# Convolution taps of the latent passes shared out anew over three engines, rope read from PSUM, Sigmoids moved to the end, and another order of the merge's products

## What is computed

```python
def conv_branch(p_glu, dw, dw_b, ln_g, ln_b, w_o):
    a, g = jnp.split(p_glu, 2, axis=-1)
    u = a * jax.nn.sigmoid(g)
    u = dwconv1d(u, dw, dw_b)              # 31 taps, depthwise, 512 channels
    u = jax.nn.silu(layernorm(u, ln_g, ln_b))
    return u @ w_o

h = modulate(rmsnorm(x, norm1_g[l]), sh1, sc1)
p = h @ w_in[l]
q, k, v = (split_heads(u) for u in jnp.split(p[..., GLU_END:QKV_END], 3, axis=-1))
q = rope_2d(q, pos_row, pos_col)
k = rope_2d(k, pos_row, pos_col)
y_conv = conv_branch(p[..., :GLU_END], ...)
y_attn = merge_heads(neighbourhood_attention(q, k, v, k_c, v_c, na_rpb[l])) @ w_na_out[l]
x = x + g1 * gated_merge(p[..., QKV_END:], y_conv, y_attn, w_out[l])   # gates: sigmoid
```

## Time and profile before

| | us |
|---|---|
| median of three executions | 2962.23 (2959.38 to 2964.63) |
| profiled execution, its own time | 2951.68 |
| its span | 2949.4 |
| TensorE busy | 2816.3 (95%) |
| VectorE busy | 1537.3 (52%) |
| ScalarE busy | 1116.2 (38%) |
| GpSimd busy | 1274.6 (43%) |

### The profile page before, as it was taken

One profiled execution on the slowest core, in us unless ns is written; L12 is line 12 of the kernel. 1 busy time (PEld: TensorE's weight loads), 2 busy tenths in 40 slices (PEclk: granted clock), 3 DMA queues, 4 the chain that ended last, 5 costly groups with the idle time before them and its releaser, 6 DMA issues.

```text
span 2949.4 us, 41217 instructions
## 1 busy us (share of the span) xinstructions
PE 2816.3 (95%) x15658; PEld 2297.0 (78%) x15658; DVE 1537.3 (52%) x1968; ACT 1116.2 (38%) x1666; POOL 1274.6 (43%) x696
## 2 busy tenths in 40 slices
PE   7999988999999999989999999999989999999998
PEld 6975734878888877867777888888877777788887
DVE  6865585353323255278775432423355867552525
ACT  4445223333323233236633422322343573342433
POOL 3444101435445173388842322222347784444443
PEclk9999998999999999999999999999999999999999
DMA  4235497323233233432222212122223222333332
GB/s 174 95 101 212 135 314 250 95 93 100 91 95 99 93 123 122 143 93 83 68 86 65 72 55 74 57 65 65 72 86 114 76 68 72 100 93 94 99 94 78
DMA packets 116008, 306.88 MB, mean 104 GB/s; under 512 B 36176, under 2 KB 44496, under 8 KB 115344
## 3 DMA queue, kind: packets, MB, share of 16 engines
q1 hardware_dynamic: 87584, 284.49, 30.5%
q10 hardware_dynamic: 27712, 18.50, 2.2%
q0 software_dynamic: 560, 1.84, 0.2%
HBM read 294.95 MB, written 7.45 MB: 103 GB/s over the span
## 4 chain that ended last, share of the span: by engine, by line
PE 77%; DVE 8%; DVEq 4%; ACT 3%; issue 2%; POOL 2%; DMA 2%; ACTq 1%; SPq 0%; POOLq 0%
PE ps L304 38%; PE ps L338 17%; PE ps L329 6%; PE ps L1941 3%; DVEq L2241 2%; POOL wlo L265 2%; DVE co L2240 2%; PE ps L2352 2%; PE ps L1945 1%; PE ps L1946 1%; PE ps L1949 1%; DMA mt<-ka 1%; PE ps L748 1%; DVE nacc L451 1%; PE ps L1999 1%
## 5 line engine op out<-in xcount | busy, mean ns | idle before, releaser
L265 POOL TENSOR_TENSOR wlo<-wraw,whi 128x1024 fp32r<-128x1024 f32 x373 | 923.1, 2484 | 1360.7 <-ACT whi L257 1359.3
L257 ACT ACTIVATE whi<-wraw 128x1024 fp32r<-128x1024 f32 x373 | 392.3, 1055 | 458.2 <-PE ps L304 170.5
L304 PE MATMUL ps<-xah,whi 128*128 128x512 f32 x992 | 387.9, 391 | 1.7 <-issue 1.7
L304 PE MATMUL ps<-xal,whi 128*128 128x512 f32 x992 | 387.4, 391 | 0.0
L304 PE MATMUL ps<-xah,wlo 128*128 128x512 f32 x992 | 280.1, 391 | 0.0
L2240 DVE SCALAR_TENSOR_TENSOR co<-ub,vec,co 128x512 f32<-128x512 f32 (+1 forms) x216 | 247.7, 1186 | 5.4 <-issue 0.4
L304 PEld LDWEIGHTS ps<-xah,whi 128*128 128x128 f32 x992 | 186.1, 188 | 42.8 <-issue 2.7
L304 PEld LDWEIGHTS ps<-xal,whi 128*128 128x128 f32 x992 | 186.1, 188 | 40.3
L304 PEld LDWEIGHTS ps<-xah,wlo 128*128 128x128 f32 x992 | 186.1, 188 | 40.2
L2339 POOL TENSOR_TENSOR co<-co,ct 128x512 f32<-128x512 f32 (+1 forms) x144 | 168.1, 1167 | 21.7 <-issue 1.8
L304 PE MATMUL ps<-hhi,whi 128*128 128x512 f32 x408 | 159.3, 390 | 1.1 <-ACT whi L257 1.1
(11 more groups left out here) (419 smaller groups left out, 6065.1 us busy)
## 6 DMA issues: line engine op xcount, KB each, us to landing
wraw<-stream SPq DMA_DIRECT2D x425, 512.0 KB, 3.5
wada<-w_ada SPq DMA_DIRECT2D x56, 512.0 KB, 7.4
wraw<-w_ada SPq DMA_DIRECT2D x40, 512.0 KB, 3.9
biasb<-attn_bias ACTq DMA_DIRECT2D x32, 256.0 KB, 3.6
xin<-x0T SPq DMA_DIRECT2D x4, 528.0 KB, 6.7
s_u<-uk ACTq DMA_DIRECT2D x8, 264.0 KB, 2.5
res<-x0T ACTq DMA_DIRECT2D x1, 2048.0 KB, 9.5
outT<-res SPq DMA_DIRECT2D x4, 512.0 KB, 2.6
```

Of the source, the lines that this page charges most:

```text
L257: act.activation(whi[:, s], wraw[:, s], ACT.Copy).then_inc(hi_done[s], 1)
L265: pool.tensor_tensor(wlo[:, s], wraw[:, s], whi[:, s].bitcast(F32), ALU.subtract).then_inc(lo_done[s], 1)
L304: last = pe.matmul(ps[:, bank, 0:b - a], w[:, s, kt], x[:, kt, c0 + a:c0 + b], start=start, stop=stop)
```

## The change

It has these parts. `rt`, the buffer of the rope's second product, is gone: the product with sin stays in PSUM bank 3 and is read from there, and the blocks between windows are written by additions of their own where they were copied. Taps in the latent passes: VectorE does tiles 1, 2 and 3 (`p.tiles`), GpSimd only adds tile 0's products, which ScalarE makes (`product_act`, into the one buffer `ct`), over all 30 taps. The context pass keeps GpSimd's two tiles. The first ten gates are read out with Copy, and their Sigmoids run in place beside the last units. The layer norm uses the bank of unit M + 3, and that unit's convolution half is begun last; in the context pass each unit now ends by itself. In `kv_act` one root moves behind a copy. TensorE gets 8 idle-time products (`keep_busy`, L505 before) at the end of the first network's S5 stage and 4 ahead of its first output projection.

```diff
@@ s5_pe
             if i in ADA_END:
                 pe.wait_ge(f_a.sem, f_a.past("bat", min(i + 2, NT - 1)))
+                if i == NT - 1:
+                    keep_busy(pe, 1, 8)
                 ada_turn(pe, ADA_END[i])
@@ class Pass
-            self.taps = KTAP if self.one else POOL_TAPS
+            self.taps = KTAP
+            self.tiles = (2, 3) if self.one else (1, 2, 3)
@@ kv_act
-        norm_root_act(act, n, then.T, "eps6")
         for j in range(4):
             ...
             act.activation(kctx[:, j], ps[:, s, 0:p.T], ACT.Copy).then_inc(acc_free[s], 1)
+            if j == 0:
+                norm_root_act(act, n, then.T, "eps6")
@@ evac_act
-            act.activation(gt[:, h, 0:p.T], a, ACT.Sigmoid).then_inc(acc_free[s], 1)
+            act.activation(gt[:, h, 0:p.T], a, ACT.Sigmoid if g >= p.U + 30 else ACT.Copy).then_inc(acc_free[s], 1)
@@ new in mix
+    def product_act(act, p, k):
+        if k > 1:
+            act.wait_ge(p.c_g.sem, p.c_g.past("conv", k - 2))
+        act.activation(ct[:, 0:p.T], ub[:, 0, k:k + p.T], ACT.Copy, scale=colr(f"dw{p.l}", 1, k * 4)).then_inc(p.c_t.sem, 1)
+    def products_of(n):
+        if n < 0:
+            return range(1, 5)
+        first = 5 + n + n // 2
+        return range(first, min(first + 1 + n % 2, KTAP))
@@ mix_act
             for g in late:
                 evac_act(act, p, g)
+            mine = list(products_of(n)) if p.lat else []
+            if mine:
+                product_act(act, p, mine[0])
             if 0 < n <= p.N:
                 copied_act(act, p, n - 1)
             if n < p.N:
                 exps_act(act, p, n)
+                if mine[1:]:
+                    product_act(act, p, mine[1])
...
         for g in range(p.U + 29, p.U + 36):
             evac_act(act, p, g)
+            d = 2 * (g - p.U - 29)
+            for h in range(d, min(d + 2, 30 - GATE0)):
+                act.activation(gt[:, h, 0:T], gt[:, h, 0:T], ACT.Sigmoid)
@@ post_dve
-            dve.tensor_tensor(rt[:, :], ps[:, 3, :], sinT, ALU.mult)
+            t = ps[:, 3, :]
+            dve.tensor_tensor(t, t, sinT, ALU.mult)
...
-                for m_, (lo, hi) in MIX.items():
-                    dve.tensor_copy(kT[:, m_ * P:m_ * P + 64], kT[:, lo * P:lo * P + 64])
-                    ins = dve.tensor_copy(kT[:, m_ * P + 64:m_ * P + P], kT[:, hi * P + 64:hi * P + P])
+                for m_, (lo, hi) in MIX.items():
+                    keys(m_ * P, 16 * (lo - 2), 8)
+                    ins = keys(m_ * P + 64, 16 * hi + 8, 8)
@@ mix_dve
         dve.wait_ge(p.c_g.sem, p.c_g.past("conv", p.taps - 2))
-        conv_taps(dve, p, range(p.taps, KTAP), (0, 1))
@@ mix_pool, latent passes
+            for n in range(-1, p.N + 2):
+                if n >= 0:
+                    split_lo(pool, p.U + 15 + n)
+                for k in products_of(n):
+                    if n < 0 and k < 4:
+                        split_lo(pool, p.U + 11 + k)
+                    o = co[:, 0, 0:T]
+                    pool.drain()
+                    pool.wait_ge(p.c_t.sem, p.c_t.past("t", k - 1))
+                    pool.tensor_tensor(o, o, ct[:, 0:T], ALU.add).then_inc(p.c_g.sem, 1)
@@ merge_pe
-        pe.wait_ge(acc_free[M % R], read_out(M - R))
+        pe.wait_ge(acc_free[(M + 3) % R], read_out(M - 1))
         conv_mean_pe(pe, p)
...
-        for kt in range(4):
-            pe.wait_ge(p.c_h.sem, p.c_h.past("hi", kt))
-            for j in range(1, R):
-                last = hi_part(j, kt)
-                if p.one and kt == 3:
-                    counted(j, last)
-            ...
-                last = hi_part(0, kt)
-                if p.one and kt == 3:
-                    counted(0, last)
+        for kt in range(2):
+            pe.wait_ge(p.c_h.sem, p.c_h.past("hi", kt))
+            for j in range(R - 1):
+                hi_part(j, kt)
+            ...
+        if p.one:
+            pe.wait_ge(p.c_h.sem, p.c_h.past("hi", 3))
+            for j in range(R):
+                for kt in range(2 if j < R - 1 else 0, 4):
+                    last = hi_part(j, kt)
+                counted(j, last)
+        else:
+            ...
+            for j in range(R - 1):
+                counted(j, lo_part(j, 3))
             for kt in range(4):
-                last = lo_part(0, kt)
-            counted(0, last)
-            for j in range(1, R):
-                counted(j, lo_part(j, 3))
+                last = lo_part(R - 1, kt)
+            counted(R - 1, last)
@@ the order of TensorE's work
             ssd_pe(pe)
+            keep_busy(pe, 5, 4)
             raw_pe(pe, U_OUT1, "ssd", ...)
```

More of the change, by code:

```diff
@@ L46 @@
 PADT = KTAP // 2
-POOL_TAPS = 22
 PHASES_DVE = 3
@@ L1830, in __init__ @@
             self.c_g = s("conv_taps", "conv", passes=self.taps - 1)
+            self.c_t = s("conv_products", "t", passes=self.taps - 1 if lat else 0)
             self.a_s, self.a_max, self.a_exp, self.a_rec, self.a_sc, self.a_turn, self.a_pt, self.a_pv = (
@@ L2142, in mix_act @@
             evac_act(act, p, g)
+            if p.lat:
+                product_act(act, p, g - p.U - 7)
+        if p.lat:
+            product_act(act, p, 4)
         late = [p.U + 8 + PRE - 1]
@@ L2167, in mix_act @@
         act.wait_ge(p.c_p.sem, p.c_p.past("var"))
-        act.activation(lst[:, 0, 0:T // P], ps[:, p.U % R, 0:T // P], ACT.Sqrt, bias=col("eps6")).then_inc(p.c_a.sem, 1)
+        act.activation(lst[:, 0, 0:T // P], ps[:, (p.U + 3) % R, 0:T // P], ACT.Sqrt, bias=col("eps6")).then_inc(p.c_a.sem, 1)
         for m in range(4):
@@ L2195, in post_dve, with keys @@
             dve.tensor_tensor(x, x, cosT, ALU.mult)
-            dve.tensor_tensor(rt[:, :], ps[:, 3, :], sinT, ALU.mult)
+            t = ps[:, 3, :]
+            dve.tensor_tensor(t, t, sinT, ALU.mult)
             dve.drain()
             if k == 0:
-                ins = dve.tensor_tensor(bycol(qT[:, :]), grid(x), grid(rt[:, :]), ALU.add)
+                ins = dve.tensor_tensor(bycol(qT[:, :]), grid(x), grid(t), ALU.add)
             else:
+                def keys(at, c, n):
+                    o = kT[:, at:at + GH * n].rearrange("p (c r) -> p c r", r=GH)
+                    return dve.tensor_tensor(o, grid(x)[:, c:c + n], grid(t)[:, c:c + n], ALU.add)
                 for a in range(2):
-                    o = kT[:, 4 * P * a:4 * P * a + 2 * P].rearrange("p (c r) -> p c r", r=GH)
-                    c = slice(32 * a, 32 * a + 32)
-                    dve.tensor_tensor(o, grid(x)[:, c], grid(rt[:, :])[:, c], ALU.add)
-                dve.drain()
+                    keys(4 * P * a, 32 * a, 32)
                 for m_, (lo, hi) in MIX.items():
-                    dve.tensor_copy(kT[:, m_ * P:m_ * P + 64], kT[:, lo * P:lo * P + 64])
-                    ins = dve.tensor_copy(kT[:, m_ * P + 64:m_ * P + P], kT[:, hi * P + 64:hi * P + P])
+                    keys(m_ * P, 16 * (lo - 2), 8)
+                    ins = keys(m_ * P + 64, 16 * hi + 8, 8)
         ins.then_inc(p.x_v.sem, 1)
@@ L2233, in out_lo_dve, with conv_taps @@
         dve.tensor_tensor(o, src, h, ALU.subtract).then_inc(p.o_v.sem, 1)
-    def conv_taps(dve, p, ks, tiles=(2, 3)):
+    def conv_taps(dve, p, ks):
         for k in ks:
-            for m in tiles:
+            for m in p.tiles:
                 o = co[:, m, 0:p.T]
@@ L2257, in mix_dve @@
             norm_in_place_dve(dve, NORM["final1"], rsrc, SEQ, g1("g_final"))
-        for m in (2, 3):
+        for m in p.tiles:
             dve.tensor_scalar(co[:, m, 0:T], ub[:, m, 0:T], colr(f"dw{l}", 1, m), colr(f"dwb{l}", 1, m), ALU.mult, ALU.add)
@@ L2308, in conv_mean_pe @@
         pe.wait_ge(p.c_v.sem, p.c_v.past("acc"))
-        pe.matmul(ps[:, p.U % R, 0:p.T], ones512, lmu[:, 0:p.T], start=True, stop=True).then_inc(p.c_p.sem, 1)
+        pe.matmul(ps[:, (p.U + 3) % R, 0:p.T], ones512, lmu[:, 0:p.T], start=True, stop=True).then_inc(p.c_p.sem, 1)
     def conv_var_pe(pe, p):
@@ L2313, in conv_var_pe @@
         for j in range(p.T // P):
-            last = pe.matmul(ps[:, p.U % R, j:j + 1], lmu[:, j * P:(j + 1) * P], ones512[:, 0:1], start=True, stop=True)
+            last = pe.matmul(ps[:, (p.U + 3) % R, j:j + 1], lmu[:, j * P:(j + 1) * P], ones512[:, 0:1], start=True, stop=True)
         last.then_inc(p.c_p.sem, 1)
@@ L2319, in conv_row_pe @@
         for j in range(p.T // P):
-            last = pe.matmul(ps[:, p.U % R, j * P:(j + 1) * P], lst[:, 1, j:j + 1].to_broadcast([P, P]), ident, start=True, stop=True)
+            last = pe.matmul(ps[:, (p.U + 3) % R, j * P:(j + 1) * P], lst[:, 1, j:j + 1].to_broadcast([P, P]), ident, start=True, stop=True)
         last.then_inc(p.c_p.sem, 1)
+    def products_of(n):
[3 more added lines that the diff above has]
+        return range(first, min(first + 1 + n % 2, KTAP))
     def mix_pool(pool, p):
@@ L2328, in mix_pool @@
         pool.wait_ge(acc_free[(p.U + 6) % R], read_out(p.U + 6))
-        for m in range(2):
+        for m in range(2 if p.one else 1):
```

(11 more changed lines are left out.)

29 lines of the change are left out of this document (16 added, 13 removed).

## The result

The changed kernel takes 2932.6 us (median of four executions, 2929.6 to 2938.3), the kernel before 2960.8 on the same chip: a ratio of 0.9907, interval 0.9886 to 0.9928, so 21 to 34 us less. A second timing on another chip gave 2932.2 against 2957.8, ratio 0.9916 (0.9901 to 0.9932).

A forecast was written before the change was run, and what follows sets the result against it. The prediction took TensorE as the bound, busy 2816.3 of 2949.4 us, with idle time and lower clock to win. Terms 1.4 - 4.6 + 3.8 - 5.2 - 6.2 - 0.3 - 1.5 = -12.6 gave median 2950; own range 2942 to 2958, overall 2936 to 2965.

The forecast's parts named there:

- VectorE is what TensorE waits for, and GpSimd holds VectorE up: Latent passes: VectorE instructions with two SBUF inputs wait until GpSimd's current instruction ends; TensorE's waits were 12.5 and 10.1 us.
- The prelude, +0.7 a pass: Before the rounds of each latent pass: added taps stall TensorE 3.6 us, sooner keys save 2.89; +1.4 for both.
- Rounds 0 to 9, the waits for `kT`, -4.6: Early rounds of both latent passes: waits for keys behind the prelude go, 2.1 us in l0 and 2.5 in l1.
- Rounds 10 to 17, +3.8 in all: Late latent rounds: six taps for four, no table loads; waits of 5.6 us a pass, plus 1.5 for lower clock.
- The convolution's sum: Behind the latent rounds: sum ready 20 us ahead of TensorE, waits of 3.3 and 0.5 go; -5.2 us with clock.
- The merge's order, -6.2: Merges of c0, l0, l1: unit M done earlier; c0 saves 3.6 and 1.6 us, l0 and l1 together 1.0.
- The products: Idle-time products in the first network: cost nothing and may keep the clock up, worth 3.0 us, half counted: -1.5.
- The moved root of `kv_act`, -0.3: In `kv_act`: one copy placed ahead of a root, saving 0.3 us.
- the first (VectorE bounds the late rounds): Late latent rounds: taps meet GpSimd's work each round, 22 us for both passes where 3.8 was counted; 2968, chance 0.15.
- the second: Prelude: a stall of 5.3 us and 6 us at the lower clock eat the gain; +4 a pass, 2958, chance 0.15.
- The third: No prelude stall (-3.6 us a pass), and the products save 5 us of lower clock from 320 on; 2938, chance 0.12.
- The fourth: Merge: the new order does nothing because loads come at the queue's own pace; +5.2 us, 2955, chance 0.05.

The follow-up runs named there:

- e3_rope: The kernel before with only the rope's product left in PSUM, additions in place of the key copies, and value copies from PSUM: 2935.6 us against 2958.1, ratio 0.9933.
- e4_taps: The kernel before with only the new share of the taps between VectorE, ScalarE and GpSimd: 2937.7 us against 2958.1, ratio 0.9942.
- p_before2: The kernel before, unchanged, profiled once more; the profiled execution took 2950.1 us.
- e2_merge: The kernel before with only the layer norm's bank and the order of the merge's products changed: 2948.8 us against 2958.1, ratio 0.9972.
- b2_late: The changed kernel with fewer taps ahead of the first post and in rounds 13 to 15: 2910.8 us against 2954.6 for the kernel before, ratio 0.9847.

## Why the prediction was right or wrong

The direction held, and what was named to show the mechanism came (no waits for `kT` and `lmu`, one for `qT`, none for the load, reciprocals of rounds 10 to 13 near 8.9 us apart, a tap at 1.0 us on the mean where I had 0.9). The size was half of the gain, and the time lies below the range. Two terms failed: the one for rounds 10 to 17 most of all, and the one for the waits for `kT`. Point by point:

- *VectorE is what TensorE waits for, and GpSimd holds VectorE up*: right, as e3_rope and e4_taps show from two sides. The rule was too narrow (below).
- *The prelude, +0.7 a pass*: nearly right. Forecast a stall of 3.6 us, measured 2.3 and 2.7, since the taps were held up less: 13.9 us for 12. A stretch at the lower clock behind the new stall, which I had left out, takes some of it back. From the end of c0 to the first scores of l0 it is 89.3 us on the mean, before and after.
- *Rounds 0 to 9, the waits for `kT`, -4.6*: the first step that failed. The 4.6 and 4.8 us of the table are won in rounds 0 to 2, where I had 2.1 and 2.5. I priced these waits at their length and left out the clock: in the first profile of before the same rounds lose 1.7 us (l0) and 2.6 (l1) more to stretches at 0.50, among them 2266 to 2272, which I had used as the price of a rival but not as something that the sum wins. And I took the waits from one profile. In another (p_before2) rounds 0 to 2 of l0 have no lower clock at all but 4.5 us of idle time where the first has 2.0, and take 30.3 us for 29.2; in the changed kernel both are gone, and they take 25.3. The windows of these rounds, before, p_before2, after:

```profile
1291.63:1320.87 29.24, 27.20 (x138) 20.11 (x137) 26.94 (x31) 13.63 (x24) 27.06 (x19) 0.94 0.33 99
```

```profile
1287.28:1317.62 30.34, 25.89 (x137) 18.90 (x137) 28.04 (x31) 13.62 (x24) 27.40 (x19) 1.00 0.30 96
```

```profile
1293.90:1319.16 25.26, 25.26 (x138) 19.13 (x137) 21.48 (x35) 18.55 (x32) 13.39 (x7) 1.00 0.30 94
```

- *Rounds 10 to 17, +3.8 in all*: the largest miss, in size and in sign. I forecast stalls of 2.1 us in round 14 and 3.5 at the end, 5.6 a pass; measured are 1.8, 0.4 behind it and, at the end, 0.9 to 1.2, in all eight passes of the changed kernel, 3.2 to 3.4 a pass in all, so that some 4.6 us of the forecast stalls never came. ScalarE's scaling in the last round came 1 us late and not 3.5. 1.5 us for a new stretch at the lower clock came, but l1 had had one already. With the sum of the convolution, two terms together: -5.7 and -4.2 against -3.1 and +1.7. That is 8.5 us of the 15.3 between forecast and table; about 2.3 of them because the first profile of before was short in just these stretches (185.8 and 175.9 for means of 186.4 and 177.6).
- *The convolution's sum*: right in kind. No wait for `lmu`, 22.7 us of room where 20 were forecast.
- *The merge's order, -6.2*: right, -5.1 in c0 for 5.2, -0.7 in l0 for 0.5.
- *The products*: forecast -1.5; nothing can be told. The moved root of `kv_act`, -0.3, was not tested by itself.
- *The median*: I carried the 10.6 us between profile and median over to the changed kernel. Its own profile lies 1.8 over its median. Executions of the kernel before lie between 2942 and 2965 us, and one profile was not enough to read an offset, or the size of waits that vary by 3 us in a pass, from it.
- *The range*: 2942 to 2958 is said to come from the bounds of prelude and late rounds, but with both at their good ends (-2.9 a pass, and -8.9 for the rounds) the same sum gives 2930. The measured 2932.6 lies inside what my own bounds allowed and outside the range that I wrote down.

Of the rivals, the first (VectorE bounds the late rounds) did not come, though half of its mechanism did: in round 13 the reciprocals are 13.8 us apart. Nor did the second. The third had the right size for the wrong reason: the prelude's stall stayed, and 320 to 330 is at 0.50 in the profile after as well. The fourth falls with e2_merge.

## What to carry to other kernels

Where a wait of some us is removed, take the stretch at the lower clock behind it as part of its price, but not from one profile: in b2_late 11.4 us of waits were worth 17.4, while in the changed kernel 21.5 us of idle time were worth 26.4 on the mean, and single profiles of before lose anything from 8.7 to 20.5 us to the lower clock. Moving work to another engine pays only if the numbers that place it are set anew: beside the rope edit the same share of taps gave nothing with 12 taps in the prelude and six in the crowded rounds, and 28 us with the taps moved to where VectorE stood idle. And judge parts in the whole kernel, alone and left out: rope and taps gave 20 and 17 us alone, and 28 at most with all the rest.

## What was unexpected of the hardware

A copy with a single input in SBUF is held up too, not only an instruction with two. VectorE in the prelude of before, GpSimd's instruction and then the copies:

```profile
1288.34 2.34 POOL L265 TENSOR_TENSOR wlo<-wraw,whi 128x1024 fp32r<-128x1024 f32 x1
```

```profile
1288.35 2.38 DVE L2208 COPY kT<-kT 128x64 f32<-128x64 f32 x1
1290.65 0.18 DVE L2207 COPY kT<-kT 128x64 f32<-128x64 f32 x1
```

The copy takes 0.18 us alone and 2.38 when GpSimd's rest of a unit starts just ahead of it; the two end together. Of the 32 copies of key blocks in the two passes 12 took 0.88 to 2.38 us and 20 took 0.18, some of these with GpSimd busy beside them throughout, so being beside it is not enough; what decides is not shown. I had taken half of what the Trainium skill says ("GPSIMD Engine Reference", Key points): it names instructions in a two-port performance mode beside those with two SBUF inputs. Whether these copies run in such a mode no run here shows. Additions with an input in PSUM kept their time: 0.25 to 0.27 us for 128x64 in e3_rope whatever GpSimd did, and copies of 128x256 from PSUM 0.41 us.

TensorE's clock differs between executions with the same waits: at a wait for `kT` of 2.9 us the first profile of before has a stretch at 0.50 from 2265.4 to 2272.2 in l1 and one of 3.4 us in l0; the second profile has one of 6.8 us, around 1284 to 1290, in l0; and the third (p_before2) has the same wait in l0 and no stretch at 0.50 there. The part of the program ahead of c0's merge took 1142.8 to 1158.8 us with no difference in its code.
